# A down projection by seven block products for eight, with GpSimd adding each pass's outputs to the residual

## The reference

```
h += W_out(concat[norm(attention), norm(short conv)])
n  = rms_norm(h, g_ffn)
h  = h + (silu(n @ w_gate) * (n @ w_up)) @ w_down        # w_down: 5632 x 2048
gate = sigmoid(rms_norm(h, g_ple) @ w_ple_gate)
h  = h + gate * (p @ w_ple_proj)
```

## Time and profile before

| | |
|---|---|
| median of 2 runs | 2502.96 us (2502.70 to 2503.22) |
| the profiled execution, device time | 2504.16 us |
| its span, first to last instruction | 2502.6 us |
| outside the span | 1.6 us |
| TensorE matmul busy | 2471.1 us (99%) |
| VectorE busy | 1708.1 us (68%) |
| ScalarE busy | 968.0 us (39%) |
| GpSimd busy | 219.1 us (9%) |
| granted TensorE clock, mean | 0.995 |

### The profile page before, as it was taken

How to read it: one execution, slowest core, us unless ns; L and a number is a source line. 1 busy time by engine, 2 the same in 40 slices (tenths; PEclk the granted TensorE clock), 3 DMA queues, 4 the chain that set the end, 5 groups by cost and what they waited for, 6 DMA issues and landing times.

```text
span 2502.6 us, 51598 instructions
## 1 busy us (share of the span) xinstructions
PE 2471.1 (99%) x20366; PEld 2456.1 (98%) x20366; DVE 1708.1 (68%) x2077; ACT 968.0 (39%) x1311; POOL 219.1 (9%) x237
## 2 busy tenths in 40 slices
PE   7999999999999999999999999999999999999998
PEld 7999999999999989999999999999999999999998
DVE  6777787778786888888888888888433323356433
ACT  5343334333433454444444444444322212233331
POOL 1120111011100000000000000000000000143000
PEclk9999999999999999999999999999999999999999
DMA  6353333333343424343343434343665443233332
GB/s 210 120 161 101 117 109 127 113 113 106 122 144 98 156 98 140 120 142 123 130 141 119 135 118 142 126 135 118 214 223 170 161 146 113 81 90 107 111 113 68
DMA packets 99887, 324.02 MB, mean 129 GB/s; under 512 B 18275, under 2 KB 18787, under 8 KB 99313
## 3 DMA queue, kind: packets, MB, share of 16 engines
q1 hardware_dynamic: 72288, 250.25, 30.6%
q0 software_dynamic: 26672, 70.69, 8.2%
q10 hardware_dynamic: 864, 2.24, 0.2%
HBM read 286.80 MB, written 40.65 MB: 131 GB/s over the span
## 4 chain that ended last, share of the span: by engine, by line
PE 83%; DVE 10%; issue 3%; DMA 2%; ACT 1%; DVEq 0%; SPq 0%; ACTq 0%
PE acc L591 15%; PE acc L595 15%; PE acc L593 15%; PE acc L795 7%; PE acc L796 7%; PE acc L794 7%; PE aux L795 5%; PE aux L794 5%; PE aux L796 5%; DVE tmp L1562 2%; DVE wlo L1330 1%; DMA wraw<-in_w_down 1%; DVE tmp L1335 1%; DVE q_both L1447 1%; ACT whi L962 1%
## 5 line engine op out<-in xcount | busy, mean ns | idle before, releaser
L1330 DVE TENSOR_TENSOR wlo<-wraw,whi 128x1024 fp32r<-128x1024 f32 (+1 forms) x276 | 333.6, 1209 | 364.3 <-ACT whi L962 363.6
L962 ACT ACTIVATE whi<-wraw 128x1024 fp32r<-128x1024 f32 (+1 forms) x276 | 285.7, 1035 | 667.6 <-PE acc L595 593.2
L591 PE MATMUL acc<-slots_a,whi 128*128 128x260 f32 x1536 | 312.8, 285 | 0.0
L595 PE MATMUL acc<-slots_a,wlo 128*128 128x260 f32 x1536 | 309.0, 282 | 0.0
L593 PE MATMUL acc<-slots_a,whi 128*128 128x260 f32 x1536 | 308.9, 283 | 0.0
L1679 DVE TENSOR_TENSOR wlo<-wraw,whi 128x1024 fp32r<-128x1024 f32 x176 | 215.2, 1223 | 104.4 <-ACT whi L1137 104.4
L591 PE MATMUL acc<-slots_b,whi 128*128 128x260 f32 x1312 | 264.3, 283 | 0.0
L593 PE MATMUL acc<-slots_b,whi 128*128 128x260 f32 x1312 | 264.0, 283 | 0.0
L595 PE MATMUL acc<-slots_b,wlo 128*128 128x260 f32 x1312 | 264.0, 282 | 0.0
L1137 ACT ACTIVATE whi<-wraw 128x1024 fp32r<-128x1024 f32 x176 | 186.2, 1058 | 155.3 <-DVE wraw L1672 83.9
L591 PEld LDWEIGHTS acc<-slots_a,whi 128*128 128x128 f32 x1536 | 238.0, 189 | 1.1 <-issue 0.5
(11 more groups left out here) (314 smaller groups left out, 5908.7 us busy)
## 6 DMA issues: line engine op xcount, KB each, us to landing
wraw<-in_w_in SPq DMA_DIRECT2D x96, 512.0 KB, 3.5
blocks<-in_w_gate SPq DMA_DIRECT2D x88, 512.0 KB, 4.1
blocks<-in_w_up SPq DMA_DIRECT2D x88, 512.0 KB, 3.7
wraw<-in_w_down SPq DMA_DIRECT2D x48, 448.0 KB, 3.5
wraw<-in_w_out SPq DMA_DIRECT2D x32, 512.0 KB, 3.5
wraw<-in_w_ple_gate SPq DMA_DIRECT2D x32, 512.0 KB, 3.5
slots_b<-f_dram SPq DMA_DIRECT2D x28, 520.0 KB, 4.6
f_dram<-sig_t POOLq DMA_DIRECT2D x22, 520.0 KB, 3.2
```

Source lines behind the costliest of these rows:

```text
L591: mm(to[:, h, :], w_h, x[:, 0, h * HALF:(h + 1) * HALF], start=begin, stop=False)
L595: done = mm(to[:, h, :], w_l, x[:, 0, h * HALF:(h + 1) * HALF], start=False, stop=end)
L962: on(whi[:, u % HILO, 0:width], wraw[:, u % RAW, 0:width], ACT.Copy).then_inc(s_whi, 1)
L1330: V.tensor_tensor(wlo[:, u % HILO, 0:width], wraw[:, u % RAW, 0:width], whi[:, u % HILO, 0:width].bitcast(F32), ALU.subtract).then_inc(s_w ...
```

## The change

The down product is done by seven block products for eight too. The 2048 outputs are 8 pairs of tiles, the 44 hidden tiles are 22 pairs, cut into six passes of 3, 4, 4, 4, 3 and 4 pairs (`PASS`). A group is one pair of output tiles in one pass: 48 groups. A group has seven units of `PASS` x 3 matmuls with 260 columns, 22 x 8 x 7 x 3 = 3696 in all. In a row, these parts change:

- **Hidden tiles.** In gate and up, VectorE makes four sums of the hidden pair's quarters (`hidden_sums`, four instructions of 260 columns) and splits seven quarters instead of four. ScalarE copies seven (`hidden_hi`, `hidden_sums_hi`). GpSimd's queue stores them in four transfers instead of two.
- **Loads.** Each group takes four blocks of `w_down` (`down_block`), and during each pass SyncE loads the next pass's hidden parts (`down_part`, 14 transfers) into the buffers that gate and up used. Their first set is loaded as the last gate/up pair frees it, ahead of group 1's block 11 in SyncE's queue.
- **Weights.** VectorE makes four block sums a group (`down_sum`) and seven low parts (`down_ahead`), ScalarE seven high parts (`down_hi_of`), 512 wide in passes of 4, 384 wide in passes of 3. They run eight units ahead (`DEEP`) of TensorE.
- **Outputs.** ScalarE copies three results and one output, VectorE forms the other three outputs from PSUM and a kept tile, all 260 wide, into one of two stages (`stage`, in `tmp`). GpSimd adds the stage, 128x1040, to a pair of residual tiles in SBUF (`hid2_pair`). The residual (16 tiles) is loaded from `h_dram` in two transfers after the last hidden pair is stored; the first addition waits for both.
- **What leaves.** The chunks, `first_copy`, `down_pair`, the reloads of single residual tiles, the additions L1888 and L1893, and GpSimd's squares. In the last pass ScalarE squares the pairs (`ple_square`) and VectorE sums them (`ple_added`), 1040 wide; the split of the finished tiles moves partly, and its VectorE half wholly, into the projection of `p`, whose results ScalarE now copies.
- The down stage is written out without loops. The scratch for GpSimd's descriptors is set to 4096.

The diff, cut to its core:

```diff
-DOWN = ((4,), (7, 7), (8, 7), (6, 5))
-CHUNKS = len(DOWN)
+PASS = (3, 4, 4, 4, 3, 4)
+PASSES = len(PASS)
+PASS_K0 = [sum(PASS[:c]) for c in range(PASSES)]
+GROUPS = KP2 * PASSES
+DEEP = 2 * HILO
+WIDE = UNIT // 2
...
+KIND_AT = (0, 2, 1, 5, 3, 4, 6)
+PART_OF = (0, 3, 1, 4, 5, 6, 2)
+BEGINS = (0, 2, 5)
+DOWN_UNITS = [(0, 0)] + [(g + (kind == 0), kind) for g in range(GROUPS) for kind in (1, 5, 2, 3, 0, 4, 6)
+                         if g + (kind == 0) < GROUPS]
+DOWN_AT = {unit: U_D + k for k, unit in enumerate(DOWN_UNITS)}
...
+    def down_source(g, kind):
+        return (down_11, down_s2, down_12, down_s1, down_22(g), down_s4, down_s3)[kind][:, 0:PASS[g // KP2] * P]
...
+        down_block(0, down_11, 0, 0, l_11)
+        down_block(0, down_21, 1, 0, l_21)
+        down_block(0, down_22(0), 1, 1, l_22[0])
+        down_block(0, down_12, 0, 1, l_12)
+        down_block(1, down_22(1), 1, 1, l_22[1])
+        for u, kind in enumerate(KIND_AT):
+            sp.wait_ge(s_unit, U_D - 7 + u + 1)
+            down_part(0, kind)
+        for g in range(1, GROUPS):
+            n = PAIRS + g
+            sp.wait_ge(s_sum, 4 * (n - 1) + 1)
+            down_block(g, down_11, 0, 0, l_11)
+            sp.wait_ge(s_wlo, DOWN_AT[g - 1, 2] + 1)
+            down_block(g, down_12, 0, 1, l_12)
+            sp.wait_ge(s_sum, 4 * (n - 1) + 4)
+            down_block(g, down_21, 1, 0, l_21)
+            if g + 1 < GROUPS:
+                sp.wait_ge(s_wlo, DOWN_AT[g - 1, 4] + 1)
+                down_block(g + 1, down_22(g + 1), 1, 1, l_22[(g + 1) % 2])
+            c, j = g // KP2, g % KP2
+            if c + 1 < PASSES and j > 0:
+                if j == 1:
+                    sp.wait_ge(s_unit, U_D + 1 + 7 * KP2 * c)
+                    pairs = PASS_K0[c + 1] + PASS[c + 1]
+                    sp.wait_ge(d_fhi, 16 * pairs)
+                    sp.wait_ge(d_flo[0], 48 * ((pairs + 1) // 2))
+                    sp.wait_ge(d_flo[1], 48 * (pairs // 2))
+                down_part(c + 1, (0, 1, 5, 2, 3, 4, 6)[j - 1])
...
+        for g, kind in DOWN_UNITS:
+            n, c, w = PAIRS + g, g // KP2, DOWN_AT[g, kind]
+            pe.wait_ge(s_wlo, w + 1)
+            if g % KP2 == 0:
+                pe.wait_ge(l_part[kind], 32 * (c + 1))
+            if kind == 0:
+                pe.wait_ge(s_0b, n - 1)
+            if kind == 1:
+                pe.wait_ge(s_q0, n + 1)
+            if kind == 5:
+                pe.wait_ge(s_1a, n - 1)
+            if kind == 2:
+                pe.wait_ge(s_11, n - 1)
+            if kind == 3:
+                pe.wait_ge(s_v2c, n + 1)
+            if kind == 4:
+                pe.wait_ge(s_p5, n + 1)
+            if kind == 6:
+                pe.wait_ge(s_1b, n + 1)
+            to, begin = banks_of(g % 2)[KIND_AT.index(kind)], kind in BEGINS
+            for p in range(PASS[c]):
+                w_h, w_l = deep(whi, w - U_D)[:, p * P:(p + 1) * P], deep(wlo, w - U_D)[:, p * P:(p + 1) * P]
+                hi, lo = (part(c, p, p + 1, PART_OF[kind]).squeeze(1) for part in (down_hi, down_lo))
+                mm(to, w_h, hi, start=begin and p == 0, stop=False, skip_group_check=not begin)
+                mm(to, w_h, lo, start=False, stop=False, skip_group_check=not begin)
+                done = mm(to, w_l, hi, start=False, stop=p == PASS[c] - 1, skip_group_check=not begin)
+            done.then_inc(s_unit, 1)
...
+        def down_hi_of(k):
+            g, kind = DOWN_UNITS[k]
+            n = PAIRS + g
+            if kind == 0:
+                act.wait_ge(l_11, 16 * (n + 1))
+            elif kind == 2:
+                act.wait_ge(l_12, 16 * (n + 1))
+            elif kind == 4:
+                act.wait_ge(l_22[n % 2], 16 * (n // 2 + 1))
+            else:
+                act.wait_ge(s_sum, 4 * n + {5: 1, 1: 2, 6: 3, 3: 4}[kind])
+            act.wait_ge(s_unit, U_D + k - DEEP + 1 if k >= DEEP else U_D - HILO + k // 2 + 1)
+            width = PASS[g // KP2] * P
+            on(deep(whi, k)[:, 0:width], down_source(g, kind), ACT.Copy).then_inc(s_whi, 1)
...
+        def ple_square(q):
+            g = (PASSES - 1) * KP2 + q
+            act.wait_ge(d_acc[g % 2], g // 2 + 1)
+            if q == 1:
+                act.wait_ge(s_p2, KP)
+            if q > 1:
+                act.wait_ge(s_pacc, q - 1)
+            on(norms[:, :, :] if q == 0 else square_t[:, :, :], hid2_pair(q), ACT.Square).then_inc(s_psq, 1)
...
+            if kind in (0, 1, 5, 6):
+                act.wait_ge(s_unit, U_D + k + 1)
+            if kind == 0:
+                act.wait_ge(s_11, n)
+                on(q0_t, to, ACT.Copy).then_inc(s_q0, 1)
+            if kind == 1:
+                act.wait_ge(s_1a, n)
+                on(v2_t, to, ACT.Copy).then_inc(s_v2c, 1)
+            if kind == 5:
+                act.wait_ge(s_1b, n)
+                on(p5_t, to, ACT.Copy).then_inc(s_p5, 1)
+            if kind == 6:
+                act.wait_ge(s_11, n + 1)
+                on(stage(g)[:, 0, HALF:T], to, ACT.Copy).then_inc(s_0b, 1)
+            if k + DEEP < D_UNITS:
+                down_hi_of(k + DEEP)
...
+        def hidden_sums(i, source, stored):
+            dve.wait_ge(s_f, i * 2 + 2)
+            if stored is not None:
+                dve.wait_ge(*stored)
+            e, o = source[:, 0, :], source[:, 1, :]
+            V.tensor_tensor(f_sums[:, 1, :], e[:, 0:HALF], e[:, HALF:T], ALU.subtract).then_inc(s_fs, 1)
+            V.tensor_tensor(f_sums[:, 3, :], e[:, HALF:T], o[:, HALF:T], ALU.subtract).then_inc(s_fs, 1)
+            dve.wait_ge(s_fs, i * 4 + 1)
+            V.scalar_tensor_tensor(f_sums[:, 0, :], o[:, HALF:T], -1.0, f_sums[:, 1, :], ALU.mult, ALU.subtract
+                                   ).then_inc(s_fs, 1)
+            dve.wait_ge(s_fs, i * 4 + 3)
+            V.tensor_tensor(f_sums[:, 2, :], o[:, 0:HALF], f_sums[:, 0, :], ALU.add).then_inc(s_fs, 1)
+        def hidden_lo(i, source):
+            dve.wait_ge(s_fs, i * 4 + 4)
+            dve.wait_ge(s_fhi, i * 2 + 1)
+            V.tensor_tensor(source[:, 0, 0:HALF].bitcast(F32R), source[:, 0, 0:HALF], f_hi[:, 0, :].bitcast(F32), ALU.subtract
+                            ).then_inc(s_flo, 1)
+            V.tensor_tensor(halves(source[:, 1, :]).bitcast(F32R), halves(source[:, 1, :]), f_hi[:, 1:3, :].bitcast(F32),
+                            ALU.subtract).then_inc(s_flo, 1)
+        def hidden_sums_lo(i):
+            dve.wait_ge(s_fhi, i * 2 + 2)
+            V.tensor_tensor(f_sums.bitcast(F32R), f_sums, f_hi[:, 3:7, :].bitcast(F32), ALU.subtract).then_inc(s_flo, 1)
...
+        def down_sum(g, kind):
+            n, width = PAIRS + g, PASS[g // KP2] * P
+            if kind == 1:
+                dve.wait_ge(l_11, 16 * (n + 1))
+                dve.wait_ge(l_21, 16 * (n + 1))
+                dve.wait_ge(l_22[n % 2], 16 * (n // 2 + 1))
+                if g == 0:
+                    dve.wait_ge(s_wlo, U_D)
+                else:
+                    dve.wait_ge(s_wlo, DOWN_AT[g - 1, 4] + 1)
+                V.tensor_tensor(down_s4[:, 0:width], down_11[:, 0:width], down_21[:, 0:width], ALU.add).then_inc(s_sum, 1)
+                dve.wait_ge(s_sum, 4 * n + 1)
+                V.tensor_tensor(down_s2[:, 0:width], down_s4[:, 0:width], down_22(g)[:, 0:width], ALU.add
+                                ).then_inc(s_sum, 1)
+            if kind == 2:
+                dve.wait_ge(l_12, 16 * (n + 1))
+                dve.wait_ge(s_sum, 4 * n + 2)
+                if g > 0:
+                    dve.wait_ge(s_wlo, DOWN_AT[g - 1, 6] + 1)
+                V.tensor_tensor(down_s3[:, 0:width], down_s2[:, 0:width], down_12[:, 0:width], ALU.add).then_inc(s_sum, 1)
+            if kind == 3:
+                V.tensor_tensor(down_s1[:, 0:width], down_21[:, 0:width], down_22(g)[:, 0:width], ALU.add
+                                ).then_inc(s_sum, 1)
+        def down_ahead(k):
+            g, kind = DOWN_UNITS[k]
+            width = PASS[g // KP2] * P
+            down_sum(g, kind)
+            dve.wait_ge(s_whi, U_D + k + 1)
+            V.tensor_tensor(deep(wlo, k)[:, 0:width], down_source(g, kind), deep(whi, k)[:, 0:width].bitcast(F32),
+                            ALU.subtract).then_inc(s_wlo, 1)
...
+        for k, (g, kind) in enumerate(DOWN_UNITS):
+            n, to = PAIRS + g, banks_of(g % 2)[KIND_AT.index(kind)]
+            if kind in (2, 3, 4):
+                dve.wait_ge(s_unit, U_D + k + 1)
+            if kind == 2:
+                dve.wait_ge(s_q0, n + 1)
+                if g >= 2:
+                    dve.wait_ge(d_acc[g % 2], g // 2)
+                else:
+                    dve.wait_ge(d_flo[g], 48 * (PAIRS // 4))
+                V.tensor_tensor(stage(g)[:, 0, 0:HALF], to, q0_t, ALU.add).then_inc(s_11, 1)
+            if kind == 3:
+                dve.wait_ge(s_p5, n + 1)
+                V.tensor_tensor(stage(g)[:, 1, HALF:T], p5_t, to, ALU.subtract).then_inc(s_1b, 1)
+            if kind == 4:
+                dve.wait_ge(s_v2c, n + 1)
```

(29 more changed lines are left out.)

419 lines of the change are left out of this document (190 added, 229 removed).

## The result

The changed kernel takes 2579.62 us (median of 2 runs, 2578.81 to 2580.43) against 2502.96: 1.0305 times the kernel before, 95% interval 1.0281 to 1.033. The forecast was 2547 within 2475 to 2590. So the direction was right and the time lies in that range, but the loss is 76.7 us where 44.5 was worked out. The forecast's own range, 2525 to 2570, was missed by 9.6 us, and the likeliest verdict was "the same" (0.59), with "slower" at 0.35.

What follows compares the result with a forecast made beforehand. TensorE, 99% busy, was taken as the bound, with VectorE to bound down after the change. Down's start and passes summed to 552.7 against 508.25, 44.5 us more: span 2547.1, median 2547 us, range 2475 to 2590.

Steps and rivals of the forecast that it cites:

- late transfers: Rival in down: block 21 lands one us late in each group, 45 us more, 2592 us; chance 0.15.
- Gain and TensorE's pace: Down: 3696 matmuls instead of 4224 at 0.1199 us each, 63.3 us gained if TensorE stays fed.
- VectorE's period: VectorE's time per group of down: 11.48 us in passes of 4, 9.72 in passes of 3, above TensorE's 10.07 and 7.55.
- an estimate of 0.2: In VectorE's group time: ScalarE's own copies of 260 columns delay one split by about 0.2 us.
- The 2.10: GpSimd's group addition alone, taken as twice a 520-wide product of 1.05 us; VectorE's loss was put at 1.95.
- Where the addition falls: Released at ScalarE's seventh copy, the addition meets VectorE with work in hand before two chained sums, so its loss is uncovered.
- the rival in which it hides in VectorE's waits: In down each addition starts while VectorE idles for ScalarE and costs 1.25 us: time 2516 us; chance 0.22.
- No exclusion: Rival in down: GpSimd's addition keeps VectorE out of nothing, TensorE sets passes of 4: 2472 us; chance 0.10.
- The start: Start of down: block 11, the last pair's VectorE work and the residual come late; TensorE resumes with unit 21 at 49.5 us.
- The first gap: Start of down: TensorE idles from 1.1 to about 7.2 us, waiting behind group 1's late block 11.
- The last pass: Pass 5 of down: 8 groups of 11.48 us plus 8.1 for additions of squares and splits of `p`, 99.9 us.
- what costs nothing: List of covered work: gate/up sums and splits, GpSimd's extra stores, the last splits and norm, written-out code, hidden-part loads.

Runs made afterwards that it cites:

- VectorE's additions: The changed kernel with all 48 residual additions made by VectorE, three units after the group's last output, instead of by GpSimd: 2543.68 us, ratio 1.0166.
- the tiny additions: The changed kernel with each of GpSimd's 48 additions cut to 8 of 520 columns of each tile, all waits kept: 2512.11 us, ratio 1.0042.
- the early start: The changed kernel with group 1's block 11 loaded ahead of the last three hidden parts and the residual in eight transfers: 2578.97 us, ratio 1.0305.
- the late stores moved: The changed kernel with four late skewed-bias stores on GpSimd's queue moved behind the load they delayed, scratch still 4096: 2558.04 us, ratio 1.0219.
- the sums run ahead: The changed kernel with VectorE's sums of two blocks one step ahead: 2552.85 us with GpSimd's additions, 2512.61 us with the additions on VectorE.

## Why the prediction was right in direction and short in size

The time lies in the range of 2475 to 2590 because that range was kept open for late transfers (2592), which did not come. The number is nearer to that rival's than to the forecast's; this is luck, by a cost that no branch had.

**Gain and TensorE's pace: right.** Where nothing holds TensorE up, groups of 4 stand 10.09 apart (10.07 worked out), and passes take 80.7.

**VectorE's period: right to 0.15 us in passes of 4, 0.34 in passes of 3.** 9.53 + 1.95 = 11.48 was forecast and 11.63 measured. The base came out as worked out, 9.52 here and again with VectorE's additions (10.67 - 1.15), though it holds an estimate of 0.2. The loss was 2.11, because most additions last 2.42 to 2.54 us and not 2.10. In passes of 3, 7.77 + 1.95 = 9.72 was forecast and 10.06 measured; the base there is 7.87 (9.02 - 1.15) and the loss 2.20. The 2.10 was twice a product whose two sources are one tile; an addition of two tiles is slower, about 2.4 us even at the start of down, where VectorE stood waiting. The trace of the kernel before has additions of two tiles, 520 wide, which the forecast did not use: 1.30 us at the shortest, twice that is 2.60. From GpSimd's timeline:

```profile
184.19 1.30 POOL L1979 TENSOR_TENSOR sums<-sums,gsq 128x520 f32<-128x520 f32 x1
```

In the passes of 4 the term was 0.15 x 24 = 3.6 us short (2.1 measured; the last groups of pass 3 already make the narrower weights of pass 4), in pass 4 0.34 x 8 = 2.7 (2.6 measured). The factor of two of the Trainium skill, "GPSIMD Engine Reference", section "Engine selection", which the forecast set aside for a row, was nearer (about 2.4 against 1.23 on VectorE): the row had the wrong form of operands.

**Where the addition falls: right.** It strikes the chain of two sums with work in hand, as argued from the release point; the rival in which it hides in VectorE's waits is out.

**No exclusion: out**, and the tiny additions show what that case is worth: 2512, or 2491 without the scratch's 21 us. Against the rival's own terms, which gave 2472, pass 0 is 11.2 longer, pass 4 6.8, pass 5 2.0 and passes 1 to 3 together 0.2.

**The start: 6.5 us short.** Pass 0 took 106.0 for 99.5. Of this, 1.7 is the longer period in the last 36 units (51.6 us for 50.0). The other 4.8 is the start itself: TensorE's unit 21, counted from 0, came at 54.3 and not 49.5. The first gap was forecast at 6.1 us and is 10.8: block 11 of group 1 was issued 2.5 us into down and not 1.3, and landed 7.5 us after that (1798.05 to 1805.55) and not 4. ScalarE's copy of it:

```profile
1805.57 0.52 ACT L1332 ACTIVATE whi<-blocks 128x384 fp32r<-128x384 f32 x1 [11.20 <-DMA blocks<-in_w_down]
```

But this gap was hidden by the wait for the residual: the first addition was to begin at 47 and began at 47.6 (1843.13 less 1795.59). What was short is the way from there to TensorE, 6.7 us for 2.5. Behind the first addition stands the second, already released, and it holds up the sum that VectorE makes ahead of its next output:

```profile
1846.02 2.28 DVE L2020 TENSOR_TENSOR wraw<-blocks 128x384 f32<-128x384 f32 x1
```

**The last pass: 2.3 us short.** 99.9 was worked out, 102.2 measured. The sum of down counts 337 units for 336, and the one too many is here (1.7 us); the longer period adds 1.2. That leaves 2.8 beyond the 8.1 for squares and `p`. Most of it is TensorE's clock, for which the forecast had no term: 66 of its matmuls followed the one before by about 0.21 us, which costs 6.2 us over the pace of 0.12, against 1.1 in pass 3. Pass 3 and pass 5 in the changed kernel, the granted clock in the third column from the end:

```profile
2088.03:2179.16 91.13, 83.52 (x671) 81.00 (x670) 79.18 (x114) 39.96 (x88) 20.54 (x8) 1.00 0.49 149
2259.58:2361.74 102.16, 87.17 (x662) 85.22 (x661) 81.48 (x112) 54.19 (x103) 20.34 (x8) 0.94 0.29 83
```

How much the clock costs differs between executions: with the early start and with the late stores moved, which leave this pass as it is, it took 99.8 and 99.6 us at a clock of 0.97, and the slower pace cost 3.9. There the squares and `p` with the clock's part come to 8.1 within 0.4 us. One wait in this pass the forecast did not have, VectorE's for the high part of the projection's weights; what it costs was not tried:

```profile
2353.98 1.22 DVE L1442 TENSOR_TENSOR wlo<-wraw,whi 128x1024 fp32r<-128x1024 f32 x1 [7.32 <-ACT whi L1021]
```

**Late transfers: out** as a mechanism of the groups: VectorE and ScalarE have no wait for a transfer from pass 1 to pass 4, and 0.55 of the DMA's time was busy in passes of 4. Such waits appear, at 0.6 to 0.7 us a group, only once the sums run ahead.

**The step that failed is the scratch.** The diff sets it to 4096 and the forecast gave it no term at all: it is neither priced nor among what costs nothing. Up to the start of down it cost 20.2 us against the same kernel without the hold-up, and 16.5 against the kernel before; the 3.7 between them lie within what two executions differ by. That is over half of the 30.2 us by which the sum of 44.5 missed 74.7. The rest is 13.4 of down (6.5, 2.1, 2.6 and 2.3, rounded) and 0.3 behind it. The scratch is named in the section on the change, and GpSimd's queue issues eight stores of 512 KB in the first 200 us, but no row of the kernel before shows what they need of it.
